# Where the split weights of the token products begin in their ring slots

## The reference

```
def sq_relu_mlp(h, w1, w2):
    return jnp.square(jax.nn.relu(h @ w1)) @ w2
```

## Time and profile before

| | |
|---|---|
| Median of three runs | 944.38 us (943.94 to 945.5) |
| Profiled execution | 945.29 us |
| Its span, first to last instruction | 943.5 us |
| TensorE busy, matmuls | 911.1 us (97% of the span) |
| TensorE busy, weight loads | 778.8 us (83%) |
| VectorE, ScalarE, GpSimd busy | 626.1, 487.4, 64.1 us |
| Mean granted TensorE clock | 0.998 |
| 512-column token matmuls, 256-column feature matmuls, 280-column token matmuls | 2,208, 1,920, 96 |

### The profile page before, as it was taken

One profiled execution on the slowest core, in us unless ns is written; L12 is line 12 of the kernel. 1 busy time (PEld: TensorE's weight loads), 2 busy tenths in 40 slices (PEclk: granted clock), 3 DMA queues, 4 the chain that ended last, 5 costly groups with the idle time before them and its releaser, 6 DMA issues.

```text
span 943.5 us, 13970 instructions
## 1 busy us (share of the span) xinstructions
PE 911.1 (97%) x5666; PEld 778.8 (83%) x5666; DVE 626.1 (66%) x1079; ACT 487.4 (52%) x732; POOL 64.1 (7%) x102
## 2 busy tenths in 40 slices
PE   7999999999999999998999999999998999999998
PEld 5787788887788888765999988887776799998887
DVE  5468988677897897775666653546677586665441
ACT  5446655555765754564655544336576365554330
POOL 3560020100010001010000000000000000000000
PEclk9999999999999999999999999999999999999999
DMA  8962255643244559460565556656453255556550
GB/s 305 251 171 96 91 155 162 156 161 131 90 135 146 181 208 268 156 156 1 161 196 181 179 180 198 203 179 200 158 200 113 90 179 182 180 188 206 182 156 23
DMA packets 80351, 154.58 MB, mean 164 GB/s; under 512 B 6679, under 2 KB 9159, under 8 KB 80288
## 3 DMA queue, kind: packets, MB, share of 16 engines
q1 hardware_dynamic: 75120, 142.81, 46.6%
q0 software_dynamic: 5024, 10.82, 5.4%
q10 hardware_dynamic: 144, 0.07, 0.0%
HBM read 152.57 MB, written 1.11 MB: 163 GB/s over the span
## 4 chain that ended last, share of the span: by engine, by line
PE 73%; DVE 13%; ACT 8%; issue 3%; DMA 2%; SPq 0%; DVEq 0%; ACTq 0%
PE ps L705 14%; PE ps L706 14%; PE ps L707 14%; PE ps L735 8%; PE ps L736 7%; PE ps L737 7%; DVE w_lo L1797 4%; ACT w_hi L1317 3%; DMA w_raw<-in_w_in 2%; PE ps L1195 1%; PE ps L1008 1%; DVE area L2143 1%; ACT y_tok L1448 1%; PE ps_mid L903 1%; PE ps_mid L917 1%
## 5 line engine op out<-in xcount | busy, mean ns | idle before, releaser
L1797 DVE TENSOR_TENSOR w_lo<-w_raw,w_hi 128x2048 fp32r<-128x2048 f32 (+1 forms) x134 | 302.3, 2262 | 193.6 <-ACT w_hi L1317 193.5
L1317 ACT ACTIVATE w_hi<-w_raw 128x2048 fp32r<-128x2048 f32 (+1 forms) x134 | 252.8, 1890 | 211.1 <-PE ps L707 146.5
L705 PE MATMUL ps<-w_hi,act_hi 128*128 128x512 f32 (+1 forms) x456 | 183.3, 402 | 5.9 <-ACT area L1335 4.1
L707 PE MATMUL ps<-w_hi,act_lo 128*128 128x512 f32 (+1 forms) x456 | 175.8, 385 | 0.0
L706 PE MATMUL ps<-w_lo,act_hi 128*128 128x512 f32 (+1 forms) x456 | 175.6, 385 | 0.0
L705 PE MATMUL ps<-w_hi,hid 128*128 128x512 f32 x296 | 116.1, 392 | 1.0 <-ACT area L1335 0.5
L706 PE MATMUL ps<-w_lo,hid 128*128 128x512 f32 x296 | 115.2, 389 | 0.0
L707 PE MATMUL ps<-w_hi,hid 128*128 128x512 f32 x296 | 115.2, 389 | 0.0
L735 PE MATMUL ps<-act_hi,w_hi 128*128 128x256 f32 x384 | 111.6, 291 | 1.0 <-ACT gate_c L1339 0.7
L736 PE MATMUL ps<-act_lo,w_hi 128*128 128x256 f32 x384 | 108.6, 283 | 0.0
L737 PE MATMUL ps<-act_hi,w_lo 128*128 128x256 f32 x384 | 108.5, 283 | 0.0
(11 more groups left out here) (363 smaller groups left out, 1259.4 us busy)
## 6 DMA issues: line engine op xcount, KB each, us to landing
w_raw<-in_ffn_w SPq DMA_DIRECT2D x64, 1024.0 KB, 5.4
w_raw<-in_w_in SPq DMA_DIRECT2D x22, 1024.0 KB, 6.2
w_raw<-in_a_w_qkv SPq DMA_DIRECT2D x18, 1024.0 KB, 5.1
w_raw<-in_b_w_qkv SPq DMA_DIRECT2D x12, 1024.0 KB, 5.1
w_raw<-in_w_out SPq DMA_DIRECT2D x8, 1024.0 KB, 5.0
w_raw<-in_b_w_o SPq DMA_DIRECT2D x4, 1024.0 KB, 5.1
w_raw<-in_w_in SPq DMA_DIRECT2D x8, 256.0 KB, 5.9
w_raw<-in_w_in SPq DMA_DIRECT2D x4, 512.0 KB, 3.8
```

The source lines that it names most:

```text
L705: pe.matmul(o, ah, wh, start=first, stop=False)
L707: mm = pe.matmul(o, al, wh, start=False, stop=last)
L1317: act.activation(w_hi[:, c % RING, :, 0:n], w_raw[:, c % RAW, :, 0:n], ACT.Copy).then_inc(w_hi_done, 1)
L1797: dve.tensor_tensor(lo, w_raw[:, c % RAW, :, 0:n], hi.bitcast(F), ALU.subtract).then_inc(w_lo_done, 1)
```

## The change

The ring of split weights gets slots of 2,080 elements (8,320 bytes) in place of 2,048 (8,192 bytes). A new function `ring` gives the 2,048 elements of a chunk in its slot: for a chunk of the token form they begin 16 elements (64 bytes) into the slot, for one of the feature form at its start. Every reader and writer of `w_hi` and `w_lo` goes through it: both splits, the head's splits, and both kinds of product. `to_line` shrinks from 120 to 24 elements. No instruction is added, removed or reordered, and no wait changes.

In addresses: `x_res`, `y_tok`, `act_hi`, `act_lo` and `w_raw` lie 384 bytes lower, `w_hi` starts at 75,392, `w_lo` at 108,672, and everything from `ident` on lies 640 bytes higher (`hid` at 144,000, the last tile's end at 229,248). All of them and all slots still begin at multiples of 128 bytes, though no longer all of 256 or 512; the token chunks alone begin at 64 past a multiple of 128.

```diff
--- before.py
+++ after.py
@@ -233,14 +233,14 @@
         rms_sum = sb("rms_sum", [128, TT])
         rden = sb("rden", [128, 4, TT])
         gate_c = sb("gate_c", [128, TT, 24])
-        sb("to_line", [128, 120])
+        sb("to_line", [128, 24])
         x = sb("x_res", [128, TT, D])
         y = sb("y_tok", [128, TT, D])
         act_hi = sb("act_hi", [128, KD, S], FR)
         act_lo = sb("act_lo", [128, KD, S], FR)
         w_raw = sb("w_raw", [128, RAW, 4, 512])
-        w_hi = sb("w_hi", [128, RING, 4, 512], FR)
-        w_lo = sb("w_lo", [128, RING, 4, 512], FR)
+        hi_room = sb("w_hi", [128, RING, 2080], FR)
+        lo_room = sb("w_lo", [128, RING, 2080], FR)
         ident = sb("ident", [128, 128])
         rope = sb("rope", [128, 2, TT, HD // 2])
         rep = sb("rep", [32, 128])
@@ -256,6 +256,12 @@
         causal = sb("causal", [128, S])
         gate_w = sb("gate_w", [128, LAYERS, 2, 2, 128])
         h_hi, h_lo = hid[:, 0], hid[:, 1]
+
+        def ring(room, c):
+
+            at = 16 if BLOCKS[CHUNKS[c][0]]["form"] == "tok" else 0
+            return room[:, c % RING, at:at + 2048].rearrange("p (k n) -> p k n", n=512)
+
 
         def cut(at, n, pattern=None, **sizes):
             v = area[:, at:at + n]
@@ -701,7 +707,7 @@
                     else:
                         ah = act_hi[:, k, 128 * half:128 * half + 128]
                         al = act_lo[:, k, 128 * half:128 * half + 128]
-                    wh, wl = w_hi[:, c % RING, k % 4, 0:n], w_lo[:, c % RING, k % 4, 0:n]
+                    wh, wl = ring(hi_room, c)[:, k % 4, 0:n], ring(lo_room, c)[:, k % 4, 0:n]
                     pe.matmul(o, ah, wh, start=first, stop=False)
                     pe.matmul(o, ah, wl, start=False, stop=False)
                     mm = pe.matmul(o, al, wh, start=False, stop=last)
@@ -728,7 +734,7 @@
                     for k in range(4 * j, 4 * j + 4):
                         if f == 0 and k % 2 == 0:
                             operand(b, 0, k)
-                        wh, wl = w_hi[:, c % RING, k % 4, cols], w_lo[:, c % RING, k % 4, cols]
+                        wh, wl = ring(hi_room, c)[:, k % 4, cols], ring(lo_room, c)[:, k % 4, cols]
                         early = k < 4 and d["use"] == "relu2"
                         ah = early_acts[:, 0, k, :] if early else act_hi[:, k, :]
                         al = early_acts[:, 1, k, :] if early else act_lo[:, k, :]
@@ -1314,7 +1320,7 @@
                         act.wait_ge(w_used, used(c - RING))
                     else:
                         act.wait_ge(acc_ready, ready(was, 1))
-                act.activation(w_hi[:, c % RING, :, 0:n], w_raw[:, c % RAW, :, 0:n], ACT.Copy).then_inc(w_hi_done, 1)
+                act.activation(ring(hi_room, c)[:, :, 0:n], w_raw[:, c % RAW, :, 0:n], ACT.Copy).then_inc(w_hi_done, 1)
 
             def hidden_hi(g):
                 act.wait_ge(h_done, g + 1)
@@ -1741,7 +1747,7 @@
             def head_hi(k):
 
                 act.wait_ge(first_in[k], 16)
-                act.activation(w_hi[:, k // 4, k % 4, :], w_raw[:, k // 4, k % 4, :], ACT.Copy).then_inc(w_hi_done, 1)
+                act.activation(ring(hi_room, k // 4)[:, k % 4, :], w_raw[:, k // 4, k % 4, :], ACT.Copy).then_inc(w_hi_done, 1)
 
             act.dma_start(ident[:, :], dram["c_ident"]).then_inc(ident_in, 16)
             for k in range(4 * HEAD):
@@ -1792,8 +1798,8 @@
                 b, j = CHUNKS[c]
                 n = BLOCKS[b]["n"]
                 dve.wait_ge(w_hi_done, split_count(c))
-                hi = w_hi[:, c % RING, :, 0:n]
-                lo = w_lo[:, c % RING, :, 0:n]
+                hi = ring(hi_room, c)[:, :, 0:n]
+                lo = ring(lo_room, c)[:, :, 0:n]
                 dve.tensor_tensor(lo, w_raw[:, c % RAW, :, 0:n], hi.bitcast(F), ALU.subtract).then_inc(w_lo_done, 1)
 
             def rsqrt(v, scale, eps, o):
@@ -2508,8 +2514,8 @@
             def head_lo(k):
 
                 dve.wait_ge(w_hi_done, k + 1)
-                dve.tensor_tensor(w_lo[:, k // 4, k % 4, :], w_raw[:, k // 4, k % 4, :],
-                                  w_hi[:, k // 4, k % 4, :].bitcast(F), ALU.subtract).then_inc(w_lo_done, 1)
+                dve.tensor_tensor(ring(lo_room, k // 4)[:, k % 4, :], w_raw[:, k // 4, k % 4, :],
+                                  ring(hi_room, k // 4)[:, k % 4, :].bitcast(F), ALU.subtract).then_inc(w_lo_done, 1)
 
             for k in range(4 * HEAD):
                 head_lo(k)
```

## The result

The changed kernel takes 951.75 us (median of 4 runs, 951.26 to 954.62) beside 944.16 us for the kernel before on the same chip (4 runs, 943.02 to 945.5). The ratio is 1.0084, with a 95% interval of 1.0065 to 1.0103: slower by 7.6 us. I had said 933.0 us, between 921 and 951. The sign is wrong, and the time lies 0.75 us outside the range.

A forecast was written before the change was run, and what follows sets the result against it. The prediction took TensorE, mainly its token products, to bound the kernel. Its terms summed to 0 + 11.4 us less, from the median of 944.38 us to 933.0 us; range 921 to 951 us, the faster case's own 922 to 941.

The forecast's parts named there:

- What bounds the kernel: TensorE, busy 911.1 of 943.5 us; in three dense stretches the token products hold 90 to 94% of the chain of waits.
- Part 1: Token matmuls of 512 columns: step falls by 6.7 ns to 220 ns, 11.4 us less over 1,710 matmuls.
- On the chain: Of 2,208 token matmuls of 512 columns, only 1,710 in the chain of waits count; all would give 14.7 us.
- Part 3: Feature matmuls: both operands stay on the 128-byte grid, step stays 120 ns, no effect.
- Part 4: Splits on ScalarE and VectorE: stay within 20 ns of 1,913 and 2,290 ns, no effect.
- Part 5: Weight DMAs into w_raw, first 45 us: between no effect and a tenth of 15.5 us, taken as none.
- Slower, by a straddled piece: Token matmuls read 17 aligned pieces: up to 13.3 ns each, 967 to 974 us; chance of slower 0.21.
- No change: Matmul surcharge belongs to fp32r or the change of stationary operand, not to addresses: 944.4 us; chance 0.26.
- What would prove me wrong: Token step unchanged, or differing with the slot (grid wider than 128 bytes), or a shorter step leaving the span unchanged.

The follow-up runs named there:

- x2: Kernel before with every tile behind to_line 64 bytes higher, so both operands of every large product move alike; 947.34 us, ratio 1.0038.
- y2: Changed kernel with all tiles other than the ring back on multiples of 512 and gate_c declared last; 949.53 us, ratio 1.0057.
- v4: y2 once more, against the kernel before; 948.07 us, ratio 1.0051.
- v2: Kernel before, unchanged, run once more; 943.99 us, ratio 1.0002.
- u1: Kernel before with only the compression weights' region of area, and what lies behind it there, 128 bytes on; 945.88 us, ratio 1.0016.
- r1: x2 with pads that return w_raw alone to a multiple of 512; 946.16 us, ratio 1.0015 to the kernel before.
- v3: Changed kernel once more, against the kernel before; 951.42 us, ratio 1.0081.
- x3: Kernel before with w_hi and w_lo alone 64 bytes higher, all other tiles in place; 940.58 us, ratio 0.9965.
- y3: y2 with slot places by form and chunk parity: token products at distance 0, feature products at 64 or 192; 935.77 us, ratio 0.991 to the kernel before.
- x1: Changed kernel without the 64 bytes, so token chunks begin at the start of their slot; 951.57 us, ratio 1.0073 to the kernel before.
- u2: y3 once more, on another chip; 932.9 us, ratio 0.9879 to the kernel before.
- x4: Kernel before with w_hi and w_lo alone 192 bytes higher, all other tiles in place; 949.77 us, ratio 1.0065.
- z3: Kernel before with w_hi and w_lo alone 128 bytes higher, slots of 8,192 bytes; 949.15 us, one execution.
- v1: y3's places in the slots with the changed kernel's other addresses (to_line of 24); 937.57 us, ratio 0.994 to the kernel before.

## Why the prediction was wrong

- **What bounds the kernel: right for the dense stretches.** There the step passes to the end in full: 1.5 and 1.7 us in the two `w2` products, as 384 x 4.3 ns say. The totals (6.1 us more busy time, 5.9 us more span) do not show it, since 3.9 of the 5.9 us are lost before 70 us, by the late start.
- **Part 1, the size and sign of the token step: wrong, and this is the step that failed.** I took 6.7 ns off, half a grid piece, between bounds of -10.0 and +13.3 ns. Measured were 229.0 and 232.9 ns in alternate slots of the down projections, 4.3 ns more than 226.7 in the mean (over all stages 231.2 against 227.5, 3.7 ns more). The failure is in how I read the earlier trace rows. From 2 ns less at 280 columns I concluded that two streams that start together disturb each other most, so that any shift would help. For 512 columns the opposite was measured: distance 0 has the lowest step of all that were tried (226.7, in x2 too). For 256 columns a shift does help: 120.0 at distance 0 falls to 113.3 at the best; why is not shown there either. One row at another width could not give the sign for this one, and I should have left the two signs nearly even.
- **"On the chain" as a multiplier: about right by the timings.** All 2,208 x 3.7 ns are 8.2 us, less some 1,920 x 0.6 = 1.2 us that the feature products gain: 7.0 us. The ring alone was timed at 5.4 us (y2) and 4.8 (v4), 0.77 and 0.69 of it; 1,710 of 2,208 are 0.77. The traces have less: behind the 240th matmul the kernel after loses 2.0 us against the first trace of the kernel before, 3.5 against v2's. That the remainder is taken up by the attention stages fits their place (there the kernel after regains 1.7 us between 356 and 446 us), but the same stretch moved by 0.9 us between two executions of the kernel before (v2), so it isn't shown.
- **Part 3, the feature step: 120.0 unchanged was wrong**, but the sign of the error stood in it: "if the grid were one of 256 or 512 bytes, they would vary from slot to slot". They do, 119.7 and 118.6. That is worth 1 us here, and it was the door to the version that wins.
- **Part 4, the splits: right.** 2,290 and 1,914 ns.
- **Part 5, the loads: w_raw itself right, the item incomplete; this is the second step that failed.** w_raw's place costs 0.05% to 0.13%, within the noise. But `to_line` moves every tile behind it, and I priced only w_raw. The compression weights, read in 256-byte runs, went from 6.6 to 8.4 us. While they are under way the 4,096-byte packets of their queue take 182 to 192 ns in the mean in the 13 traces with this region on the grid, 228 in u1, and 237 to 254 in the six with everything off it (in r1 all but w_raw); the 2,048-byte packets of the weight loads have a median of 84 ns in every trace, wherever w_raw starts. The Trainium skill, DMA: Bandwidth & Descriptors, How a descriptor splits into AXI transactions, has a transaction start at a multiple of 256 bytes; by that a 256-byte piece off the grid would need two and not one, a 2,048-byte piece nine and not eight. The traces agree in direction and order: a clear effect on the transfer with the short runs, none that can be told on the long pieces. That this is the reason isn't shown, since the trace has no transactions and no 256-byte packets for this transfer. Everything off the grid together, w_raw included, costs 3.7 us in x2, where no step changed, and the kernel after some 2.2 us (7.6 less y2's 5.4) to 3.4 us (v3 less v4), though the intervals of these ratios overlap.
- **The sum as measured:** ring 4.8 to 5.4 us, other tiles 2.2 to 3.4 us, together 7.0 to 8.8; the change cost 7.6.
- **The rivals.** "Slower, by a straddled piece", with half a piece 956 us, had the right sign, a size of the right order (4.3 of 13.3 ns, where half a piece is 6.7), and the wrong mechanism: in x2 every operand is at 64 past the grid and no step grows. "No change" falls with the steps. It rested also on the Trainium skill, TensorE: Matmul & The Clock Gate, Part 2, step 1, by which loading the next weights takes nothing from the running matmul's reads and the operands' relative place can't matter. In these runs it does matter, from 226.7 to 233.3 ns for 512 columns and from 113.3 to 120.0 for 256. For fp32r with a load beside each matmul the measurement decides against that consequence; whether the reads themselves disturb each other no run shows.
- **What would prove me wrong** was named and came: the step differs with the slot, so the grid is wider than 128 bytes.

**Open.** Why the step depends on the distance: a collision of the two reads would fit, but no run sees the reads. Why x3 and y3 have two steady values at one distance, and why x1 has 227.3 ns and not 226.7 in its slots at distance 0 in the down projections (228.2 against 227.5 over all stages); one suspect is what the slot before left, and it was not tried. And what makes the start late off the grid, and how much of it is the compression weights' (v4 and u2, on the grid, were late by 2.2 and 1.8 us as well), and so how the 7.6 us divide: by the medians most of it is the ring's, by the trace of the kernel after most of it is the start's.

## What to carry to other kernels

The start addresses of the two operands of an fp32r matmul, taken against each other modulo 256 bytes, are a setting of their own: measure it for each shape and form, since the best distance tried here for 512 moving columns (0) is the worst for 256. When a tile's size changes, list every tile declared behind it and its transfers by piece length, not only the tile that the change is about. A surcharge seen in a trace says that something is there to gain, not in which direction to move; where one row at another shape gives the sign, take both signs as about equally likely.

## What the runs showed of the hardware that I had not expected

Steps at full granted clock, with a weight load beside each matmul, in the two feed-forward parts (`w2` products for 512 columns, `w1` products for 256):

| distance | 512 columns, ns | 256 columns, ns |
|---|---|---|
| 0 | 226.7 (227.3 in x1) | 120.0 (119.9 in the kernel after) |
| 32 | 233.3 | 116.7 |
| 64 | 229.0 (after), 228.9 or 233.3 (x3) | 117.8 (x4), 113.3 or 117.7 (y3) |
| 128 | 233.0 (x1), 232.1 to 232.7 (z3) | 118.6 |
| 192 | 232.9 (after), 233.3 (x4) | 113.3 or 117.8 (x3), 113.3 or 117.7 (y3) |
| 224 | 233.3 | 118.3 |

- The absolute place doesn't matter in the two cases tried: 226.7 and 120.0 ns with all operands 64 bytes on (x2), and y3's steps again with everything 128 bytes past a multiple of 256 (v1).
- The step is a state that holds for whole stages, not a scatter about a mean, and it carries over from one form to the other: x3 stays at 117.8 and then 233.3 ns through the first feed-forward part, at 113.3 and then 228.9 through the second.
- The compression weights, 512 KB read in 256-byte runs, land in 8.0 to 8.7 us when they are written at 64 or 128 past a multiple of 256 (7 traces), and in 6.5 to 7.2 us at a multiple of it (13 traces).
